# Loads, modulation and the first projections of a two-layer block as one program block on one Trainium2 core

## The chip, the core and the metric

The kernel runs on one core of one Trainium2 chip. The metric is the device time of one execution, in microseconds (us). The engines go by their names in the profile: PE (TensorE, matrix products; PEld is its weight load), DVE (VectorE), ACT (ScalarE), POOL (GpSimd) and SP (SyncE, which here issues all loads).

## The reference, cut to what matters

The program computes a whole model of two blocks (attention with a short convolution, a gated recurrence, then a second block of attention and feed-forward parts). The change is in its first 100 us: the modulation vectors of layer 0, the modulation of 512 tokens of x and of 256 context tokens, and the first projections.

```python
mod = silu(c) @ w_ada + b_ada          # per layer; the same for c_ctx
def modulate(h, shift, scale):
    return h * (1 + scale) + shift

def ab_layer(x, xc, mod, mod_c, w_in, w_out, sink, conv_w, ln_g, ln_b, row, col, ctx_out):
    shift, scale, gate = jnp.split(mod, 3, axis=-1)
    shift_c, scale_c, gate_c = jnp.split(mod_c, 3, axis=-1)
    q, k, v, g_a, xb, b_g, c_g, g_b = split_cols(modulate(x, shift, scale) @ w_in, widths)
    hc = modulate(xc, shift_c, scale_c)
    qc, kc, vc, g_ac, xbc, b_gc, c_gc, g_bc = split_cols(hc @ w_in, widths)
    ...
    x_new = layer_norm(DEEPNORM_ALPHA * x + gate * y, ln_g, ln_b)
```

(The line of `mod` is put in words of the same form; the rest is the reference's.) Shift and scale are needed before the first projection, `gate` only behind the output projection.

## The kernel before, in words

**Layout.** Activations lie with the 1024 model columns on partitions: 8 tiles (k = 0 to 7) of 128 partitions, each with 768 tokens (512 of x, 256 of context). A weight unit is 128x2048 f32 (1 MB); of `w_in` it holds two output tiles of 128 columns.

**Products in three parts.** Each f32 operand is split in a high part, rounded by ACT (`split_high`), and a low part, the difference, by DVE (`split_low`). `product3` (L276 to L280) issues three matmuls: high by high, low by high, high by low. In a weight unit's split (`SplitStream`, L262 and L268) the operands are 128x2048, in an x tile's (`SplitTiles`, L288 and L291) 128x768. PE waits for the low part of a unit before its first tile.

**Stage 1, `stage_start` (L366).** SP issues v, cf, eight units of the ada weights (u = 0 to 7, into a ring of five places), the first unit of `w_in`, x and context in four chunks of two tiles each, four more ada units (u = 8 to 11) and the second unit of `w_in`. PE multiplies the twelve ada units (L423, 8 products of 32 weight columns by 256 each) and after every second unit turns a row of 512 results to partitions (`flip`, L412, four small products), from rows that ACT copied out of PSUM (`turn`, L441). Units 0 to 7 are shift and scale, 8 to 11 are `gate`. When the fourth flip is there, DVE adds the bias (L475), adds 1 to the scale (L487), splits the low part of the first `w_in` unit (L270), and then modulates: for each of 8 tiles one instruction of 128x512 for x and one of 128x256 for context (L494), with the low split of the tile before (L293) between. ACT makes the high parts (L289), and then multiplies X by ALPHA (L456, eight of 128x768). The last DVE instruction is the bias of `gate`.

**Stage 2, `stage_ab_in` (L503).** A list `tiles` sets PE's order: q 0 to 3, k, v, then ga, rotations "r", xb, cg, gb, bg. Tile i uses PSUM banks 2(i mod 4) and the next, and waits until tile i-4 has been taken out. A tile other than v runs all eight k of x (24 matmuls of 128x512), then all eight of the context (24 of 128x256). ACT takes q, k, v, ga, xb and gb out (L581), and one iteration ahead splits the next unit; DVE does rotations, cg and bg, and casts a constant block (L632). SP loads further units when a raw place is free.

**Between them** stands the end of one `nc.Block()` and the start of the next: every engine jumps to the next block when all have ended theirs. The rows of the trace call what ends that wait "PEq L383".

Of the kernel before, what the change touches and what calls it, by code (L numbers as in the profile page):

```python
# [90 lines left out]
class Sems:  # L91

    def __init__(self, nc, es, tag):
# [67 lines left out]
        assert len(self.range) == 62  # L161


def program(nc, d):
# [5 lines left out]
    with es:  # L170
# [181 lines left out]
        raw_cb = arena1[:, ab_mark:ab_mark + NCB]  # L352
# [13 lines left out]
        def stage_start():  # L366
# [3 lines left out]
            S, N = stage_sems()  # L370
            c = Carve(0, arena1)
# [4 lines left out]
            padded_, picks_ = c(KT * 32), c(2)  # L376
            cond_ = padded_.rearrange("p (k x) -> p k x", k=KT)
            rows = [ca[:, 0:512], ca[:, 512:1024]]
            arrived = w_arrived[7:12]
            chunks = [slice(2 * i, 2 * i + 2) for i in range(4)]  # L380
            tiles_in = SplitTiles(S, [yin[:, k, :] for k in range(KT)], xh, xl)

            with nc.Block() as block:  # L383
                @block.sync
                def _(sp):
                    def unit(u):
                        if u >= 5:
                            sp.wait_ge(S.used, u - 4)
                        sp.dma_start(ring[u % 5], d["w1"][U0["ada0"] + u]).then_inc(arrived[u % 5], 16)

                    sp.sem_clear(N.range)
                    sp.sem_clear(w_range)
                    sp.dma_start(v1[:, :], d["v1"]).then_inc(S.load, 16)
                    sp.dma_start(cf[:, :], d["cf"]).then_inc(S.load2, 16)
                    for u in range(8):
                        unit(u)
                    ab_stream.fetch(sp, src_ab, 0)
                    for i, ks in enumerate(chunks):
                        sp.dma_start(X[:, ks, 0:L], d["xT"][:, ks, :]).then_inc(x_arrived[i], 16)
                        sp.dma_start(X[:, ks, L:T], d["ctxT"][:, ks, :]).then_inc(x_arrived[i], 16)  # L400
                    for u in range(8, 12):
                        unit(u)
                    ab_stream.fetch(sp, src_ab, 1)
                    sp.wait_ge(S.load, 16)
                    sp.wait_ge(S.load2, 16)

                @block.tensor
                def _(pe):
                    def flip(b):
                        pe.wait_ge(S.act_out, b + 1)  # L410
                        for j in range(4):
                            last = nc.tensor.matmul(PS[:, 6 + b // 4, 8 * b + 2 * j:8 * b + 2 * j + 2],  # L412
                                                    rows[b % 2][:, j * P:(j + 1) * P], picks_, start=True, stop=True)
                        last.then_inc(S.flipped, 1)

                    for u in range(12):
                        pe.wait_ge(arrived[u % 5], 16 * (u // 5 + 1))
                        if u == 0:
                            pe.wait_ge(S.act_step, 1)
                        w = ring[u % 5].rearrange("p (k n) -> p k n", k=KT)  # L420
                        for k in range(KT):
                            g = slice(32 * (k % 4), 32 * (k % 4) + 32)
                            last = nc.tensor.matmul(PS[g, u // 2, (u % 2) * 256:(u % 2 + 1) * 256],  # L423
                                                    cond_[:, k, :], w[:, k, :], start=(k < 4), stop=(k >= 4))
# [5 lines left out]
                        if u == 7:  # L430
                            flip(3)
# [3245 lines left out]
```

## Time and profile before

| what | value |
|---|---|
| median of 3 runs | 2468.87 us (2467.23 to 2468.99) |
| the profiled execution's own time | 2468.88 us |
| its span | 2467.1 us |
| PE busy | 2275.9 us, 92% of the span |
| DVE, ACT, POOL busy | 60%, 44%, 11% |
| mean granted clock of TensorE | 0.971 of full speed |
| first of 40 slices (61.7 us each) | PE 5 tenths, clock 7 tenths, DMA 8 tenths, 344 GB/s |

The profiled execution stands at the median of the runs, and its own time is 1.8 us above its span. Share of busy time says where an engine is used; what sets the length of a stretch is read from its waits and its order.

### The profile page before, as it was taken

How to read it: one execution, taken by the hardware profiler on the slowest of the kernel's cores; microseconds unless marked ns; L12 is line 12 of the kernel's file. 1: busy time of each engine (PE TensorE's matmuls, PEld its weight loads, DVE VectorE, ACT ScalarE, POOL GpSimd, SP SyncE). 2: the span in 40 equal slices, each digit the busy share in tenths (PEclk: the TensorE clock that was granted, in tenths of full speed). 3: DMA queues.
4: the chain of work that ended last, by engine and by line, in shares of the span. 5: the costliest groups of instructions: out<-in, count | busy, mean ns of one | idle time of the engine just before them, and what ended most of it. 6: DMA issues, size and time to landing. Idle time of an engine off the chain costs nothing. (4 is left out here: it accounts for less than half of the span.)

```text
span 2467.1 us, 36146 instructions
## 1 busy us (share of the span) xinstructions
PE 2275.9 (92%) x15278; PEld 1875.4 (76%) x15278; DVE 1470.0 (60%) x2225; ACT 1085.9 (44%) x1728; POOL 275.1 (11%) x147
## 2 busy tenths in 40 slices
PE   5999889789999978798899999999998899999997
PEld 3988767578888867677588888886786588888876
DVE  3133484748797795547667666347457667666255
ACT  3111373547667673435634334244336634334253
POOL 0000101513223150101001000001101010000011
PEclk7999999889999998899999999999999999999999
DMA  8112105311111112231022222331230012222321
GB/s 344 73 52 69 35 2 196 112 58 48 60 52 52 52 61 91 87 120 35 5 94 86 103 103 86 111 114 57 91 132 18 18 69 86 103 102 86 111 103 52
DMA packets 35201, 205.19 MB, mean 83 GB/s; under 512 B 3936, under 2 KB 5472, under 8 KB 14816
## 3 DMA queue, kind: packets, MB, share of 16 engines
q1 hardware_dynamic: 35040, 202.88, 23.2%
q8 instruction: 121, 1.98, 0.3%
q14 instruction: 40, 0.33, 0.0%
HBM read 200.77 MB, written 2.10 MB: 82 GB/s over the span
## 5 line engine op out<-in xcount | busy, mean ns | idle before, releaser
L278 PE MATMUL ps<-a_high,w_high 128*128 128x512 f32 (+1 forms) x1680 | 627.5, 373 | 38.5 <-DVE a_low L2550 18.6
L279 PE MATMUL ps<-a_low,w_high 128*128 128x512 f32 (+1 forms) x1680 | 619.1, 369 | 0.0
L280 PE MATMUL ps<-a_high,w_low 128*128 128x512 f32 (+1 forms) x1680 | 618.6, 368 | 0.0
L278 PEld LDWEIGHTS ps<-a_high,w_high 128*128 128x128 f32 x1680 | 318.2, 189 | 102.1 <-issue 18.4
L2168 DVE TENSOR_TENSOR w_low<-raw_ring,w_high 128x2048 fp32r<-128x2048 f32 x102 | 234.9, 2303 | 262.6 <-ACT w_high L2162 257.9
L279 PEld LDWEIGHTS ps<-a_low,w_high 128*128 128x128 f32 x1680 | 318.4, 190 | 53.6 <-issue 1.4
L280 PEld LDWEIGHTS ps<-a_high,w_low 128*128 128x128 f32 x1680 | 318.3, 189 | 52.7
L2162 ACT ACTIVATE w_high<-raw_ring 128x2048 fp32r<-128x2048 f32 x102 | 195.3, 1915 | 369.2 <-PE ps L280 282.0
L278 PE MATMUL ps<-x_high,place_high 128*128 128x512 f32 (+1 forms) x704 | 251.6, 357 | 9.9 <-POOL place_low L270 7.9
L279 PE MATMUL ps<-x_low,place_high 128*128 128x512 f32 (+1 forms) x704 | 246.0, 349 | 0.0
L280 PE MATMUL ps<-x_high,place_low 128*128 128x512 f32 (+1 forms) x704 | 245.4, 349 | 0.0
L278 PEld LDWEIGHTS ps<-x_high,place_high 128*128 128x128 f32 x704 | 135.4, 192 | 30.1 <-POOL place_low L270 8.8
L2964 POOL TENSOR_TENSOR arena<-arena 128x512 f32<-128x512 f32 (+1 forms) x36 | 56.3, 1563 | 865.4 <-ACT arena L3169 788.4
L279 PEld LDWEIGHTS ps<-x_low,place_high 128*128 128x128 f32 x704 | 135.5, 192 | 17.0 <-issue 0.7
L280 PEld LDWEIGHTS ps<-x_high,place_low 128*128 128x128 f32 x704 | 135.1, 192 | 17.4
L270 POOL TENSOR_TENSOR place_low<-place_raw,place_high 128x1024 fp32r<-128x1024 f32 x40 | 111.7, 2798 | 287.7 <-ACT place_high L266 287.7
L3421 DVE TENSOR_TENSOR arena<-ps,arena 128x1024 f32<-128x1024 f32 x44 | 53.9, 1224 | 133.3 <-PE ps L280 133.2
L3256 ACT ACTIVATE arena<-arena 128x512 f32<-128x512 f32 x44 | 27.9, 634 | 157.9 <-DVE arena L3443 157.9
L278 PE MATMUL ps<-x_high,ab_high 128*128 128x256 f32 (+1 forms) x256 | 87.9, 343 | 0.7 <-PEq L698 0.7
L279 PE MATMUL ps<-x_low,ab_high 128*128 128x256 f32 (+1 forms) x256 | 86.2, 337 | 0.0
L280 PE MATMUL ps<-x_high,ab_low 128*128 128x256 f32 (+1 forms) x256 | 86.1, 336 | 0.0
L2775 ACT ACTIVATE arena<-ps,arena 128x128 f32<-128x128 f32 (+3 forms) x128 | 66.0, 534 | 43.4 <-DVE arena L2828 43.1
(393 smaller groups left out, 4043.8 us busy)
## 6 DMA issues: line engine op xcount, KB each, us to landing
raw_ring<-w_dram SPq DMA_DIRECT2D x110, 1024.0 KB, 4.9
arena<-w_dram SPq DMA_DIRECT2D x26, 1024.0 KB, 8.1
place_raw<-wc_dram SPq DMA_DIRECT2D x48, 512.0 KB, 3.6
place_raw<-w_dram SPq DMA_DIRECT2D x11, 1024.0 KB, 5.0
ab_raw<-w_dram SPq DMA_DIRECT2D x10, 1024.0 KB, 4.9
x<-xT_dram SPq DMA_DIRECT2D x4, 512.0 KB, 13.9
out_dram<-x SPq DMA_DIRECT2D x1, 2048.0 KB, 7.2
arena<-r_dram SPq DMA_DIRECT2D x2, 992.0 KB, 6.0
```

The costliest lines, as they stand in the source:

```text
L270: (nc.gpsimd if by_pool else nc.vector).tensor_tensor(self.low(n), self.raw(n), self.high(n).bitcast(f32), O.subtract)\
L278: nc.tensor.matmul(out, wh, xh, start=start, stop=False)
L279: nc.tensor.matmul(out, wh, xl, start=False, stop=False)
L280: return nc.tensor.matmul(out, wl, xh, start=False, stop=stop)
L2162: nc.scalar.activation(self.high(n), self.raw(n), A.Copy).then_inc(w_hi, 1)
L2168: nc.vector.tensor_tensor(self.low(n), self.raw(n), self.high(n).bitcast(f32), O.subtract)\
L2775: last = nc.scalar.activation(pr[:, u % 3, g, c_ * w:(c_ + 1) * w], region(u)[:, g, c_ * w:(c_ + 1) * w], A.Exp, bias=st_bias[:, u, i:i + ...
L2964: nc.gpsimd.tensor_tensor(sq[:, 0:2, ts], sq[:, 0:2, ts], sq[:, k:k + 2, ts], O.add)\
L3256: nc.scalar.activation(hc[:, j % 2, 0, :], hc[:, j % 2, 0, :], A.Silu)\
L3421: nc.vector.tensor_tensor(hs[:, j % 2, :, :], tile2(PAIR[j % 4]), rstd[:, 1, :].unsqueeze(1).to_broadcast([P, 2, L]), O.mult)\
```

## The change

The two stages become one block, `stage_ab_in`. In it:

- The list of tiles is now q0, q1, q2, "m", q3, "f", k, v, and the rest as before. "m" is the products of ada units 8 to 11 (`gate`), into the two PSUM banks of its place in the list, from which ACT copies 128x1024 into `mod_rows`; "f" is their two flips, and DVE adds the bias.
- q0 and q1 are computed together, k outermost: when the low part of x tile k is there, PE does for both tiles the three 512-token and the three 256-token products of that k.
- DVE modulates x only. It does tiles 0 and 1, then the low split of the first `w_in` unit, then the low split of tile 0, and goes on with tile 2. ACT modulates the context (`context`, an Identity with scale and bias, 128x256), one tile ahead of its high split.
- The eight multiplications by ALPHA go among the evictions of the first projections, two for each of tile places 1 to 4.
- SP issues the second `w_in` unit ahead of ada units 8 to 10; unit 11 has a place inside the modulated tiles 4 to 6 and waits until all eight tiles are split; the third unit of `w_in`, and the constants `ca` and `sink`, come before it, the constant `cb` behind it. `cb` lies where the modulated tiles 0 to 3 were, so ACT waits for its cast before it writes ga 0.
- A set of twelve semaphores (`FirstSems`, `F`) serves what was stage 1.

```diff
-        def stage_start():
+        def stage_ab_in():
             S, N = stage_sems()
+            F = FirstSems(nc, es)
...
+            gate_place = arena1[:, yin_at + 4 * T:yin_at + 4 * T + UNIT]
+            places = [(ring[u % 5], u % 5, u // 5 + 1) for u in range(8)]
+            places += [(ring[3], 3, 2), (ring[4], 4, 2), (ring[2], 2, 3), (gate_place, 0, 3)]
...
+            tiles = ([("q", j) for j in range(3)] + [("m", 0), ("q", 3), ("f", 0), ("k", 0), ("v", 0), ("ga", 0), ("r", 0), ("ga", 1), ("r", 1),
...
                     ab_stream.fetch(sp, src_ab, 0)
                     for i, ks in enumerate(chunks):
                         sp.dma_start(X[:, ks, 0:L], d["xT"][:, ks, :]).then_inc(x_arrived[i], 16)
                         sp.dma_start(X[:, ks, L:T], d["ctxT"][:, ks, :]).then_inc(x_arrived[i], 16)
-                    for u in range(8, 12):
-                        unit(u)
                     ab_stream.fetch(sp, src_ab, 1)
...
+                    for u in (8, 9, 10):
+                        unit(u, (4, 5, 8)[u - 8])
                     ab_stream.load(sp, src_ab, RAW, RAW + 1)
                     sp.dma_start(ca, d["ca"]).then_inc(S.load, 16)
                     sp.dma_start(nsink, d["sink"]).then_inc(S.load, 16)
+                    sp.wait_ge(F.operand, KT)
+                    unit(11, 6)
                     sp.dma_start(raw_cb, d["cb"]).then_inc(S.load2, 16)
                     ab_stream.load(sp, src_ab, RAW + 1, 13 + RAW + 1)
...
+                    for k in range(KT):
+                        tiles_in.tile(pe, k)
+                        for i in range(2):
+                            ns = slice(i * P, (i + 1) * P)
+                            for a, b in ((0, L), (L, T)):
+                                last = product3(wide(i)[:, a:b], wh[:, k, ns], wl[:, k, ns], xh[k][:, a:b], xl[k][:, a:b],
+                                                k == 0, k == KT - 1)
...
+                        if t[0] == "m":
+                            for u in range(8, 12):
+                                last = mod_unit(u, 2 * (i % 4) + (u - 8) // 2)
+                            last.then_inc(S.pe_tile, 1)
+                            continue
+                        if t[0] == "f":
+                            pe.wait_ge(S.act_out, count(("m", 0)))
+                            flip(4, 2 * (i % 4))
+                            flip(5, 2 * (i % 4)).then_inc(S.pe_tile, 1)
+                            continue
...
+                    def context(k):
+                        if k % 2 == 0:
+                            act.wait_ge(x_arrived[k // 2], 32)
+                        nc.scalar.activation(yin[:, k, L:T], X[:, k, L:T], A.Identity, bias=modv(0, 0, 1, k),
+                                             scale=modv(0, 1, 1, k)).then_inc(F.kept, 1)
...
+                    ab_stream.split_high(act, u0)
+                    act.wait_ge(F.mixed, 1)
+                    context(0)
+                    for k in range(KT):
+                        if k < KT - 1:
+                            context(k + 1)
+                        act.wait_ge(F.kept, k + 1)
+                        act.wait_ge(F.dve_out, k + 1)
+                        tiles_in.split_high(act, k)
...
+                        if 1 <= i < 5:
+                            for k in range(2 * i - 2, 2 * i):
+                                nc.scalar.mul(X[:, k, :], X[:, k, :], ALPHA)
...
-                    ab_stream.split_low(dve, 0)
-                    for k in range(KT + 1):
-                        if k < KT:
-                            if k % 2 == 0:
-                                dve.wait_ge(x_arrived[k // 2], 32)
-                            for who, (a, b) in enumerate(((0, L), (L, T))):
-                                nc.vector.tensor_scalar(yin[:, k, a:b], X[:, k, a:b], modv(0, 1, who, k),
-                                                        modv(0, 0, who, k), O.mult, O.add).then_inc(S.dve_out, 1)
-                        if k:
-                            tiles_in.split_low(dve, k - 1)
+                    for k in range(KT + 1):
+                        if k < KT:
+                            if k % 2 == 0:
+                                dve.wait_ge(x_arrived[k // 2], 32)
+                            nc.vector.tensor_scalar(yin[:, k, 0:L], X[:, k, 0:L], modv(0, 1, 0, k), modv(0, 0, 0, k),
+                                                    O.mult, O.add).then_inc(F.dve_out, 1)
+                        if k == 1:
+                            ab_stream.split_low(dve, u0)
+                        if k:
+                            tiles_in.split_low(dve, k - 1)
```

**Place 1: DVE, from the scale's added 1 to the second x tile's low part.** `place_low` is the low part of the first `w_in` unit, `arena<-x,mod` a modulation. Before, and then in the changed kernel:

```order
L487 TENSOR_SCALAR mod<-mod 128x16
L270 TENSOR_TENSOR place_low<-place_raw,place_high 128x2048
L494 TENSOR_SCALAR arena<-x,mod 128x512
L494 TENSOR_SCALAR arena<-x,mod 128x256
L494 TENSOR_SCALAR arena<-x,mod 128x512
L494 TENSOR_SCALAR arena<-x,mod 128x256
L293 TENSOR_TENSOR x_low<-arena,x_high 128x768
```

```order
L632 TENSOR_SCALAR mod<-mod 128x16
L638 TENSOR_SCALAR arena<-x,mod 128x512 x2
L292 TENSOR_TENSOR place_low<-place_raw,place_high 128x2048
L315 TENSOR_TENSOR x_low<-arena,x_high 128x768
L638 TENSOR_SCALAR arena<-x,mod 128x512
L315 TENSOR_TENSOR x_low<-arena,x_high 128x768
```

The weight unit's low split moved behind two modulations, and those of the context left DVE.

**Place 2: PE, at the start of the projections and around "m".** Before, the last flips, the jump to the next block and the first products:

```order
L423 MATMUL ps<-arena 32x256 x32
L412 MATMUL ps<-arena 128x2 x8
L383 UNCONDITIONAL_BRANCH
L539 UNCONDITIONAL_BRANCH
L278 MATMUL ps<-x_high,place_high 128x512
L279 MATMUL ps<-x_low,place_high 128x512
L280 MATMUL ps<-x_high,place_low 128x512
```

In the changed kernel the start, and then the place of "m" between q2 and q3:

```order
L476 MATMUL ps<-arena,padded 32x256 x8
L482 MATMUL ps<-picks,arena 128x2 x4
L300 MATMUL ps<-x_high,place_high 128x512
L301 MATMUL ps<-x_low,place_high 128x512
L302 MATMUL ps<-x_high,place_low 128x512
L300 MATMUL ps<-x_high,place_high 128x256
```

```order
L302 MATMUL ps<-x_high,ab_low 128x256
L476 MATMUL ps<-arena,padded 32x256 x32
L300 MATMUL ps<-x_high,ab_high 128x512
L301 MATMUL ps<-x_low,ab_high 128x512
L302 MATMUL ps<-x_high,ab_low 128x512
```

The four `gate` units and both jumps left the front of the projections; the units stand behind the third projection tile.

**Place 3: SP, from the last chunk of context on.** Before, and then in the changed kernel:

```order
L400 DMA x<-ctxT_dram 128x2x256
L389 DMA arena<-w_dram 128x2048 x4
L251 DMA ab_raw<-w_dram 128x2048
L383 UNCONDITIONAL_BRANCH
L529 UNCONDITIONAL_BRANCH
L531 ISA
L251 DMA place_raw<-w_dram 128x2048
L533 DMA arena<-ca_dram 128x1024
L534 DMA arena<-sink_dram 128x8
L535 DMA arena<-cb_dram 128x2560
```

```order
L453 DMA x<-ctxT_dram 128x2x256
L273 DMA ab_raw<-w_dram 128x2048
L442 DMA arena<-w_dram 128x2048 x3
L273 DMA place_raw<-w_dram 128x2048
L458 DMA arena<-ca_dram 128x1024
L459 DMA arena<-sink_dram 128x8
L442 DMA arena<-w_dram 128x2048
L462 DMA arena<-cb_dram 128x2560
```

The second `w_in` unit moved ahead of the `gate` units, and the last of these behind the third `w_in` unit and two constants.

## Rows read from the trace of the kernel before

**Rows 1.** PE's waits from 53 to 262 us: engine, line, waited for, total, times, longest.
```profile
PE ps L278 <- PEq L383: 1.3, 1, 1.3
```

**Rows 2.** Busy time by stretch: length, PE, PEld, DVE, ACT, POOL, clock, DMA share, GB/s.
```profile
53.60:72.10 18.50, 18.45 (x96) 16.07 (x97) 2.29 (x1) 2.72 (x2) 0.00 (x0) 0.90 0.55 215
72.10:262.00 189.90, 189.90 (x1128) 167.74 (x1127) 55.89 (x51) 33.89 (x28) 0.00 (x0) 1.00 0.18 62
```

**Rows 3.** Timeline of PE, 20 to 73 us: start, length, work, idle before.
```profile
20.13 1.05 PE L412 MATMUL ps<-arena 128*128 128x2 f32 x8
...
24.22 1.07 PE L423 MATMUL ps<-arena 128*32 128x256 f32 x16 [2.04 <-DMA arena<-w_dram]
25.22 1.05 PE L412 MATMUL ps<-arena 128*128 128x2 f32 x8
...
29.21 1.87 PE L412 MATMUL ps<-arena 128*128 128x2 f32 x8 [0.72 <-ACT arena L441]
40.47 1.93 PE L423 MATMUL ps<-arena 128*32 128x256 f32 x16 [9.39 <-DMA arena<-w_dram]
...
50.48 1.87 PE L412 MATMUL ps<-arena 128*128 128x2 f32 x8 [0.52 <-ACT arena L441]
53.65 0.76 PE L278 MATMUL ps<-x_high,place_high 128*128 128x512 f32 x1 [1.30 <-PEq L383]
...
63.77 0.40 PE L278 MATMUL ps<-x_high,place_high 128*128 128x512 f32 x1
...
72.11 0.40 PE L278 MATMUL ps<-x_high,ab_high 128*128 128x512 f32 x1
```

**Rows 4.** Timeline of DVE, 31 to 38 us.
```profile
31.19 0.19 DVE L475 TENSOR_TENSOR mod<-ps,v 128x32 f32<-128x32 f32 x1 [25.18 <-PE ps L412]
...
31.62 2.29 DVE L270 TENSOR_TENSOR place_low<-place_raw,place_high 128x2048 fp32r<-128x2048 f32 x1
33.83 1.64 DVE L494 TENSOR_SCALAR arena<-x,mod 128x512 f32<-128x512 f32 x4
35.60 0.96 DVE L293 TENSOR_TENSOR x_low<-arena,x_high 128x768 fp32r<-128x768 f32 x1
36.48 0.87 DVE L494 TENSOR_SCALAR arena<-x,mod 128x512 f32<-128x512 f32 x2
37.26 0.95 DVE L293 TENSOR_TENSOR x_low<-arena,x_high 128x768 fp32r<-128x768 f32 x1
```

**Rows 5.** DMA queue of SP, 16 to 33 us: start and length of issues.
```profile
16.63 0.47 SPq L400 DMA_DIRECT2D x<-ctxT_dram  x1
...
27.98 1.09 SPq L400 DMA_DIRECT2D x<-ctxT_dram  x1
...
32.35 0.43 SPq L251 DMA_DIRECT2D ab_raw<-w_dram  x1
```

**Rows 6.** DMA issues at 16.6 us: count, KB each, us to landing.
```profile
x<-ctxT_dram SPq DMA_DIRECT2D x1, 256.0 KB, 15.0
```

**Rows 7.** DMA issues at 28.0 us, the same columns.
```profile
x<-ctxT_dram SPq DMA_DIRECT2D x1, 256.0 KB, 10.0
```

**Rows 8.** DMA issues at 32.4 us, the same columns.
```profile
ab_raw<-w_dram SPq DMA_DIRECT2D x1, 1024.0 KB, 18.0
```

**Rows 9.** Timeline of ACT, 28 to 50 us.
```profile
29.05 1.91 ACT L266 ACTIVATE place_high<-place_raw 128x2048 fp32r<-128x2048 f32 x1
34.73 1.62 ACT L289 ACTIVATE x_high<-arena 128x768 fp32r<-128x768 f32 x2 [3.77 <-DVE arena L494]
...
46.91 3.03 ACT L456 ACTIVATE x<-x 128x768 f32<-128x768 f32 x4
```

**Rows 10.** ACT groups by shape over the span: an activation with a scale operand.
```profile
L1785 ACT ACTIVATE x<-x,v 128x256 f32<-128x256 f32 x16 | 8.1, 587 | 3.5 <-DVE x L1623 3.5
```

**Rows 11.** Busy time by stretch, as in the second group, where the clock rises.
```profile
56.00:57.00 1.00, 1.00 (x4) 0.81 (x3) 1.00 (x1) 0.00 (x0) 0.00 (x0) 0.50 0.99 401
57.00:58.00 1.00, 1.00 (x5) 0.77 (x5) 0.86 (x1) 0.00 (x0) 0.00 (x0) 0.90 0.98 410
```

More of the change, by code:

```diff
@@ L161, in __init__, with sem @@
         assert len(self.range) == 62
+class FirstSems:
+    def __init__(self, nc, es):
+        def sem(name):
+            return es.enter_context(nc.semaphore(f"{name}_first"))
+        self.load = sem("load")
+        self.load2 = sem("load2")
+        self.ready = sem("ready")
+        self.used = sem("used")
+        self.act_step = sem("act_step")
+        self.act_out = sem("act_out")
+        self.flipped = sem("flipped")
+        self.mixed = sem("mixed")
+        self.dve_out = sem("dve_out")
+        self.kept = sem("kept")
+        self.rms_high = sem("rms_high")
+        self.operand = sem("operand")
 def program(nc, d):
@@ new lines, in flip, with first_flip @@
+                    def flip(b, bank):
+                        for j in range(4):
+                            last = nc.tensor.matmul(PS[:, bank, 8 * b + 2 * j:8 * b + 2 * j + 2],
+                                                    rows[b % 2][:, j * P:(j + 1) * P], picks_[:, :], start=True, stop=True)
+                        return last
+                    def first_flip(b):
+                        pe.wait_ge(F.act_out, b + 1)
+                        flip(b, 6).then_inc(F.flipped, 1)
+                    for u in range(8):
+                        if u == 0:
+                            pe.wait_ge(F.act_step, 1)
+                        mod_unit(u, u // 2).then_inc(F.used, 1)
+                        if u == 2:
+                            pe.wait_ge(F.ready, 2)
+                        if u % 2 == 0 and u >= 2:
+                            first_flip(u // 2 - 1)
@@ new lines, in _ @@
+                    first_flip(3)
+                    ab_stream.ready(pe, u0)
+                    wh, wl = [w.rearrange("p (k n) -> p k n", k=KT) for w in (ab_stream.high(u0), ab_stream.low(u0))]
+                    for k in range(KT):
[5 more added lines that the diff above has]
+                                                k == 0, k == KT - 1)
+                            if k == KT - 1:
+                                last.then_inc(S.pe_tile, 1)
@@ L541, in _ @@
                     for i, t in enumerate(tiles):
+                        if i < 2:
+                            continue
                         if i >= 4:
```

181 lines of the change are left out of this document (75 added, 106 removed).

## The prediction

> **What bounds the kernel now.** I read the waits of PE first, over the stage of the projections. From 53 to 262 us PE waits once, 1.3 us, and that is the jump into the block [rows 1]; from 72.1 us to 262 us it is busy 189.90 of 189.90 us at full clock [rows 2]. So this stage is a solid block of PE work: it ends earlier by what it starts earlier, and later by each microsecond of work put into it. Nothing else there has a say, since ACT is busy for 33.89 us and DVE for 55.89 us of the 189.90.
>
> Then the timeline of PE ahead of it. The last flip that shift and scale need starts at 29.21 us and takes 1.87 us, so DVE has them at 31.19 us; after it PE waits 9.39 us for an ada unit, works through the four `gate` units at their pace of arrival, and begins the first projection at 53.65 us [rows 3]. Between 31.1 and 53.65 us PE does only work that nothing in the projections needs. What the projections need comes from DVE and ACT. On DVE the reader is to see that the low part of x tile 0, the last thing that a first product needs, would be there at 35.60 + 0.96 = 36.56 us [rows 4], 17 us before PE looks at it.
>
> **The change, part by part.**
>
> *Start of the projections.* In the new order of DVE the shift and scale are ready at 31.62 us, as before. x tile 0 has landed at 16.63 + 15.0 = 31.63 us [rows 5, 6], so it isn't late by more than a hair. Two modulations of 128x512: four instructions, two of 512 and two of 256, took 1.64 us [rows 4]; with the two short ones gone I take 0.95 us (bounds 0.82, half of it, and 1.64). Then the weight unit's low part, 31.62 to 33.83 = 2.21 us from start to start, then the low part of tile 0, 0.96 us [rows 4]. 31.62 + 0.95 + 2.21 + 0.96 = 35.74 us, and with 0.1 us for the signal to PE **35.85 us** (35.7 to 36.6). ACT isn't the last here: its high part of the weight unit ends at 30.96 us [rows 9]; then come two contexts, each 0.59 us at most [rows 10], and one high part, 0.81 us (two took 1.62) [rows 9]: 31.6 + 1.18 + 0.81 = 33.6 us, hidden by DVE's 2.21 us. The start moves from 53.65 to 35.85: **-17.8 us**. The 1.30 us of the jump [rows 3] are in this term.
>
> *q0 and q1 by tiles of x.* The same 96 matmuls in another order, so their price is that of the two tiles before, 72.11 - 53.65 = 18.46 us; the second alone took 72.11 - 63.77 = 8.34 us [rows 3]. The difference is the low clock at the start: 0.50 in the stretch from 56 to 57, 0.90 in the next [rows 11]. It stays as it is if PE is again fed without a gap. PE wants at full clock 2 x 8.34 / 8 = 2.09 us for each x tile. DVE now gives one per modulation plus low part, at most 0.55 + 0.96 = 1.5 us (with the context in it, it was 37.26 - 35.60 = 1.66 us [rows 4]); ACT one per 0.59 + 0.81 = 1.4 us [rows 9, 10]. Both are shorter than 2.09. The last chunk of x lands at 27.98 + 10.0 = 38.0 us [rows 5, 7], and tile 6 is not modulated before 35.74 + 4 x 1.4 = 41.3 us. So **0**; bounds: 1.8 us less where the clock were full at once (18.46 - 16.68), 1.8 us more where the low stretch were twice as long. q2 would begin at 35.85 + 18.46 = 54.3 us.
>
> *The gate's work amid the projections.* It used to stand in a gap and now stands in solid PE work, so all of it counts. Four units: at full clock one started at 24.22 and the flips behind it at 25.22, so 1.00 us each [rows 3]. Two flips of four products, 1.05 us each [rows 3]. 4.0 + 2.1 = **+6.1 us**. At the low clock the rows say 1.93 us and 1.87 us [rows 3]: 11.5 us, the upper bound. I take the low price, as the engine comes out of 27 us of unbroken matmuls. Does PE wait there? "m" begins at 54.3 + 8.34 = 62.6 us. Unit 11 is the late one: behind x at 38.0 us there are ahead of it five units and `ca`, 5.8 MB, at 401 to 410 GB/s [rows 11] 14.2 us: 52.2 us, and 2.6 us for itself, 54.8 us. Its own wait, for all tiles split, ends at 35.74 + 7 x 1.4 = 45.5 us. So 7.8 us are to spare. "f" waits for ACT's copy of 1024 columns, with the whole of q3 (8.34 us) to hide in.
>
> *Second and third `w_in` unit.* The second landed at 32.35 + 18.0 = 50.4 us behind four `gate` units [rows 5, 8]. Even so late, 1.91 us of ACT [rows 9] and 2.29 us of DVE [rows 4] make 54.6 us against 54.3 us wanted; moved ahead of three of those units it lands some 8 us earlier. 0. The third is wanted at "k", 54.3 + 8.34 + 4.0 + 8.34 + 2.1 = 77.1 us, and ACT may split it from the end of q1 on. 0. Queued behind SP's new wait (until 45.5 us) are unit 11, `cb` and the fourth `w_in` unit, which is not read before ga 0, some 30 us later. 0.
>
> *ACT's multiplications by ALPHA.* Eight of 0.8 us (3.03 for four [rows 9]) move from beside the gate units to beside q1 to q3, where ACT has 0.8 us of eviction and 1.9 us of splitting per 8.34 us tile: 1.6 + 0.8 + 1.9 = 4.3. Tile i waits only for tile i-4. 0. The context halves on ACT are hidden as shown, and the cast of `cb` and its wait before ga 0 have DVE's idle time. 0.
>
> **Sum:** -17.8 + 6.1 = -11.7 us. Span 2467.1 - 11.7 = 2455.4, and 1.8 us around it, **2457.2 us**. The profiled execution (2468.88) stands at the median of the runs (2468.87), so no correction. Behind the stage all waits are on other engines, not on a time of day; the shift goes through whole.
>
> **The rivals.**
>
> *Gate's group dear.* The small products are at the low clock's price, or PE stops at the seams: -17.8 + 11.5 = -6.3, so 2462.6 us. For it: such units ran at either price in this trace. Against: each at the high price in the rows shown came after idle time of 0.52 to 9.39 us, and here none is due. 8%.
>
> *PE starved tile by tile, with the clock low (slower).* Place: q0 and q1, where PE now waits eight times for DVE. If modulation, context, high and low part run one behind another, 0.55 + 0.59 + 0.81 + 0.96 = 2.9 us a tile, PE at full clock (2.09 us) would wait 0.8 us each time, and the granted clock may stay at 0.50, as it does at 56 us [rows 11]. The point from which it decides is a supply above 2.09 us. At half clock the two tiles cost up to 33.4 us instead of 18.46 (+14.9), and "m" and "f" still low 5.4 more: -11.7 + 14.9 = +3.2 to +8.6, thus 2472.1 to 2477.5 us. For it: products that came in bursts, at 40.47 and 50.48 us, were at the low price [rows 3]. Against: the contexts run a tile ahead on another engine, and DVE did its longer list in 1.66 us a tile with ACT's high part beside it. At the low clock PE wants up to twice 2.09 us a tile, so it isn't starved there, and it is then fed as it was at 53.65 us. 4%. The Trainium skill, TensorE: Matmul & The Clock Gate, section on HAM oscillation, describes this pattern: an engine that waits for the next operand in each step along the contraction falls back to the slow clock and starts every step cold. By that rule the change would land in this rival; the trace has no such step-by-step feed with full-size products, so no row shows it.
>
> *Code and operands arrive late under a full DMA queue.* PE now starts while the queues move over 400 GB/s [rows 11], until about 57 us; before, the DMA share over q0 and q1 was 0.55 [rows 2]. Each such stop I price like the 1.30 us of the jump [rows 3]; two or three give 2460 to 2461 us. For it: instruction queues move in this program too, and share the DMA engines. Against: nothing of the kind stops PE in the stage before [rows 1]. 7%. The Trainium skill, Runtime: NRT & Kernel Launch, section Instruction fetch mechanics, says that an engine's code comes by its own DMA queue and is mostly hidden when sequential, while a taken jump out of the loaded pages stalls; by it this rival would cost nothing. No row here shows a fetch under load on PE while it is saturated.
>
> *The change gives nothing:* a later wait takes it all, 2468.9 us. PE's waits leave no room for it in this stage [rows 1, 2]. 2%.
>
> **How the numbers follow.** Forecast 79%, gate dear 8%, late code 7%, starved 4%, nothing 2%. The range reaches from the forecast less 1.8 us of clock and 0.9 us of run to run scatter, 2454.5, up to 2461.5, which takes in the clock's 1.8 us upward, 0.75 us of a later start and the third rival. A measurement of this kernel tells 0.2%, 4.9 us, from no change. Faster: 79 + 8 + 7 = 94, less 1 for mishaps added up: 93%. Same 3%, slower 4%.
>
> **What would show it.** First full-size product at 35.7 to 36.6 us; q2 at about 54.3; clock at full from about 40 us on; x tiles' low parts 1.3 to 1.5 us apart; 32 columns' products for `gate` in 4 us at about 62.6 us with no wait; no PE wait from 36 us to the stage's end, near 250 us. Wrong, if PE idles between x tiles, if the clock column reads 0.5 beyond 42 us, if "m" waits for unit 11, or if the stage ends at 262 us as before.

## The result and the profile after

| | before | changed |
|---|---|---|
| median | 2468.93 us (4 runs, 2467.23 to 2469.44) | 2455.86 us (4 runs, 2450.82 to 2456.95) |
| ratio | | 0.9943, 95% interval 0.9928 to 0.9958 |
| profiled execution | 2468.88 us, span 2467.1 | 2455.45 us, span 2453.6 |
| PE busy | 2275.9 us, 92% | 2270.5 us, 93% |

The changed kernel is 13 us faster, 0.57%. The forecast was 2457.2 us, in a range of 2454.5 to 2461.5. (In the three later sets of runs the kernel before had medians of 2467.1 to 2467.7 us, so 1 to 2 of the 13 us may be the scatter of these four runs.)

PE's waits from 30 to 252 us in the changed kernel (columns as in [rows 1]):

```profile
PE ps L300 <- DVE x_low L315: 4.8, 1, 4.8
PE ps L482 <- ACT arena L560: 0.7, 1, 0.7
```

Both lie ahead of the first projection. In the projections PE waits for nothing, as before [rows 1], and as the forecast needed: no wait between x tiles, none at "m" for unit 11, none at "f". The timeline of PE gives the places:

```profile
24.19 1.94 PE L476 MATMUL ps<-arena,padded 128*32 128x256 f32 x16 [1.89 <-DMA arena<-w_dram]
26.05 1.87 PE L482 MATMUL ps<-picks,arena 128*128 128x2 f32 x8
27.85 1.93 PE L476 MATMUL ps<-arena,padded 128*32 128x256 f32 x16
30.50 1.87 PE L482 MATMUL ps<-picks,arena 128*128 128x2 f32 x8 [0.72 <-ACT arena L560]
37.14 0.77 PE L300 MATMUL ps<-x_high,place_high 128*128 128x512 f32 x1 [4.77 <-DVE x_low L315]
...
55.48 0.40 PE L300 MATMUL ps<-x_high,ab_high 128*128 128x512 f32 x1
...
63.91 3.66 PE L476 MATMUL ps<-arena,padded 128*32 128x256 f32 x64
67.50 0.50 PE L300 MATMUL ps<-x_high,ab_high 128*128 128x512 f32 x1
...
75.99 1.84 PE L482 MATMUL ps<-picks,arena 128*128 128x2 f32 x16
77.69 0.49 PE L300 MATMUL ps<-x_high,place_high 128*128 128x512 f32 x1
```

The first full-size product starts at 37.14 us and not at 53.65 [rows 3]: 16.5 us earlier. q0 and q1 take 55.48 - 37.14 = 18.34 us, where they took 18.46. The gate's products take 67.50 - 63.91 = 3.59 us and its flips 77.69 - 75.99 = 1.70 us, 5.3 us together. 16.5 + 0.1 - 5.3 = 11.3 us.

The full price of the gate's work is a little higher. From the start of the third projection tile (55.48 us here, 72.11 before) to the first row of the attention stage (275.93 and 286.91 us, shown below) it is 220.45 us, against 214.80 before: 5.65 us. The part that the rows above don't show, 0.36 us, lies around them: the first product behind each group takes 0.50 and 0.49 us in place of 0.40. With it the sum closes: 16.51 + 0.12 - 5.65 = 10.98 us.

DVE shows how PE is fed:

```profile
32.48 0.19 DVE L619 TENSOR_TENSOR mod<-ps,v 128x32 f32<-128x32 f32 x1 [26.46 <-PE ps L482]
...
32.92 1.00 DVE L638 TENSOR_SCALAR arena<-x,mod 128x512 f32<-128x512 f32 x2
33.84 2.29 DVE L292 TENSOR_TENSOR place_low<-place_raw,place_high 128x2048 fp32r<-128x2048 f32 x1
36.04 0.95 DVE L315 TENSOR_TENSOR x_low<-arena,x_high 128x768 fp32r<-128x768 f32 x1
36.91 0.54 DVE L638 TENSOR_SCALAR arena<-x,mod 128x512 f32<-128x512 f32 x1
37.37 0.95 DVE L315 TENSOR_TENSOR x_low<-arena,x_high 128x768 fp32r<-128x768 f32 x1
```

Low parts come 37.37 - 36.04 = 1.33 us apart, against the 1.66 us of before [rows 4] and the 2.09 us that PE wants. ACT carries the context beside it (timeline of ACT):

```profile
38.30 0.59 ACT L565 ACTIVATE arena<-x,mod 128x256 f32<-128x256 f32 x1
38.87 0.84 ACT L311 ACTIVATE x_high<-arena 128x768 fp32r<-128x768 f32 x1
```

**Where the last 2 us came from.** The profiled spans differ by 13.5 us, not 11.3. The first row of PE in the later blocks tells where. Before:

```profile
286.91 2.00 PE L714 MATMUL ps<-arena 64*128 64x256 f32 x16 [2.36 <-PEq L528]
383.16 0.47 PE L278 MATMUL ps<-x_high,ab_high 128*128 128x512 f32 x1 [0.65 <-PEq L698]
...
1140.44 1.16 PE L2716 MATMUL ps<-arena 64*128 64x128 f32 x16 [1.96 <-PEq L2251]
```

Changed:

```profile
275.93 3.63 PE L769 MATMUL ps<-arena 64*128 64x256 f32 x16 [2.36 <-PEq L435]
369.81 0.47 PE L300 MATMUL ps<-x_high,ab_high 128*128 128x512 f32 x1 [0.65 <-PEq L753]
...
1126.78 1.16 PE L2770 MATMUL ps<-arena 64*128 64x128 f32 x16 [1.96 <-PEq L2305]
```

The attention stage starts 10.98 us earlier. It then took 96.25 us before and 93.88 us here, with the same instructions. The busy time by stretch shows the clock in it, before and then changed:

```profile
294.91:302.91 8.00, 6.87 (x30) 4.26 (x30) 6.62 (x20) 4.68 (x23) 0.01 (x1) 0.50 0.00 0
```

```profile
283.93:291.93 8.00, 6.18 (x36) 3.35 (x34) 6.96 (x22) 5.32 (x25) 0.00 (x0) 0.86 0.00 0
```

Before, 8 us of the stage's ragged start ran at 0.50; in the changed kernel the same place had 0.86. That difference belongs to the two executions and not to the change, as the experiments show: the same stretch, from the attention stage's start to the block that starts at 1140.44 us before, took 853.5 us before, 850.9 in the changed kernel, and between 847.3 and 854.6 us in the profiles of the twelve runs below, none of which touches it. What follows that stretch took 1326 to 1327 us each time. So about 11 us are the change's, and a single execution adds or takes some 3 us. (That the clock makes all of this variation isn't shown; the 8 us above are one place where it differs.)

### The profile page after: what moved, and what is told of

The parts are those of the page before. It is cut to its first block and busy times, and to the rows that moved or that the text cites. A ratio compares the mean times of both kernels' runs of the same rounds, so it can differ in the third digit from the quotient of the medians.

```text
span 2453.6 us, 36142 instructions
## 1 busy us (share of the span) xinstructions
PE 2270.5 (93%) x15278; PEld 1872.6 (76%) x15278; DVE 1468.0 (60%) x2217; ACT 1089.7 (44%) x1735; POOL 274.9 (11%) x147
## 5 line engine op out<-in xcount | busy, mean ns | idle before, releaser
L2829 ACT ACTIVATE arena<-ps,arena 128x128 f32<-128x128 f32 (+3 forms) x128 | 66.0, 534 | 43.5 <-DVE arena L2882 43.2
```

Of the source, the lines that this page charges most:

```text
L2829: last = nc.scalar.activation(pr[:, u % 3, g, c_ * w:(c_ + 1) * w], region(u)[:, g, c_ * w:(c_ + 1) * w], A.Exp, bias=st_bias[:, u, i:i + ...
```

## The experiments

Two theories at the start. **A:** the projections are one solid block of PE work, and the end moves with its start and with what is put into it. **B:** the gain is something else, the jump, or the going by x tiles alone, or the gate's move alone. "q2" is the start of the third projection tile, the attention stage's start is that of the rows above. "q0, q1 whole" takes back the going by x tiles and keeps the gate's move; "gate in front" takes back the gate's move and keeps the going by tiles. Ratios are to the kernel before on the same chip.

| run | median, us | ratio, 95% interval | first full-size product | q2 | attention stage |
|---|---|---|---|---|---|
| before | 2468.93 | | 53.65 | 72.11 | 286.91 |
| changed | 2455.86 | 0.9943 (0.9928 to 0.9958) | 37.14 | 55.48 | 275.93 |
| changed, again | 2455.05 | 0.9951 (0.9939 to 0.9963) | 37.18 | 56.82 | 277.27 |
| q0, q1 whole | 2466.12 | 0.9999 (0.9987 to 1.0010) | 46.16 | 65.36 | 285.81 |
| gate in front | 2467.91 | 0.9998 (0.9985 to 1.0010) | 53.69 | 72.13 | 286.93 |
| both undone | 2466.53 | 1.0000 (0.9991 to 1.0009) | 53.96 | 70.74 | 285.54 |
| context on DVE | 2456.92 | 0.9962 (0.9948 to 0.9977) | 36.79 | 56.40 | 276.84 |
| no gate products | 2452.27 | 0.9935 (0.9919 to 0.9952) | 37.08 | 55.38 | 271.99 |
| second unit late | 2455.29 | 0.9955 (0.9940 to 0.9970) | 37.11 | 55.29 | 275.73 |
| fill | 2454.76 | 0.9950 (0.9933 to 0.9967) | 35.82 | 52.83 | 273.27 |
| fill, again | 2454.46 | 0.9945 (0.9932 to 0.9957) | 35.68 | 54.18 | 274.62 |
| low part in pieces | 2454.34 | 0.9946 (0.9931 to 0.9961) | 35.76 | 55.05 | 275.50 |
| pieces and 3 fills | 2456.99 | 0.9955 (0.9940 to 0.9970) | 34.97 | 53.68 | 274.13 |
| pieces and 4 fills | 2453.93 | 0.9942 (0.9930 to 0.9954) | 35.78 | 53.54 | 274.00 |

The last two columns give a ruler that the clock doesn't blur: from q2 to the attention stage it is 214.80 us in the three kernels with the gate's work in front, 220.44 to 220.46 us in the ten that have it inside, and 216.61 us without its products. So the products cost 3.84 us there, the flips 1.81, and what else differs between executions lies ahead of q2 or behind the attention stage's start.

### q0 and q1 whole

```diff
-                    for k in range(KT):
-                        tiles_in.tile(pe, k)
-                        for i in range(2):
-                            ns = slice(i * P, (i + 1) * P)
-                            for a, b in ((0, L), (L, T)):
+                    tiles_in.tile(pe, KT - 1)
+                    for i in range(2):
+                        ns = slice(i * P, (i + 1) * P)
+                        for a, b in ((0, L), (L, T)):
+                            for k in range(KT):
...
```

> q0 and q1 are computed one after the other, once all eight tiles of x are split; everything else as changed. Theory (the start of PE's solid block sets the end): the low part of the last x tile ends at 46.0 us in the changed kernel, so the first full-size product moves from 37.1 to about 46.1 us, PE then has no wait, and the time is 9 us above the changed kernel's 2455.9, about 2464.8 us. Rival (the gain came from the gate's work and the jump, not from going by tiles): within 2 us of the changed kernel.

Measured 2466.12 us. Its timeline of PE:

```profile
46.16 0.76 PE L300 MATMUL ps<-x_high,place_high 128*128 128x512 f32 x1 [13.78 <-DVE x_low L315]
```

PE waits 13.78 us for the last x tile in place of 4.77 for the first: 9.0 us, as forecast, and the attention stage starts 9.9 us later (0.9 us of it is a longer stretch at the low clock: q0 and q1 took 65.36 - 46.16 = 19.20 us). The theory holds, and by its median the whole gain of the change is gone.

### The gate in front again

```diff
-            places += [(ring[3], 3, 2), (ring[4], 4, 2), (ring[2], 2, 3), (gate_place, 0, 3)]
+            places += [(ring[3], 3, 2), (ring[4], 4, 2), (ring[2], 2, 3), (ring[1], 1, 3)]
...
-            tiles = ([("q", j) for j in range(3)] + [("m", 0), ("q", 3), ("f", 0), ("k", 0),
+            tiles = ([("q", j) for j in range(3)] + [("q", 3), ("k", 0),
...
                     first_flip(3)
+                    for u in range(8, 12):
+                        mod_unit(u, 4 + (u - 8) // 2).then_inc(F.used, 1)
+                    for b in (4, 5):
+                        pe.wait_ge(F.act_out, b + 1)
+                        flip(b, 7).then_inc(F.flipped, 1)
```

Unit 11 is issued with units 8 to 10, and ACT takes the two rows out inside and behind its high parts, as before the change.

> The gate's four units and its flips go back in front of the first projection, inside the one block; x still goes by tiles. Theory: PE waits for the landing of unit 11 (about 48 us), flips by about 52 us, first full-size product near 52.5 us and not 37.1 us: 15.4 us later, and 5.3 us less inside the projections, so 10 us above the changed kernel, about 2466 us. The rest to the 2468.9 us of before, 1 to 3 us, is the jump. Rival (going by tiles is what gave the time): near 2456 to 2460 us.

Measured 2467.91 us. Its timeline of PE:

```profile
43.44 1.94 PE L475 MATMUL ps<-arena,padded 128*32 128x256 f32 x16 [10.28 <-DMA arena<-w_dram]
...
50.88 1.07 PE L475 MATMUL ps<-arena,padded 128*32 128x256 f32 x16 [1.42 <-DMA arena<-w_dram]
51.89 1.95 PE L481 MATMUL ps<-picks,arena 128*128 128x2 f32 x16
53.69 0.76 PE L300 MATMUL ps<-x_high,place_high 128*128 128x512 f32 x1
```

PE goes through the four units at their pace of arrival; the last comes at 50.88 us and not near 48, so the first product comes 1.2 us later than expected. It waits for loads that it doesn't need, and starts where it did before the change. Again the whole gain is gone. Nothing is left between this kernel and the one before (286.93 and 286.91 us at the attention stage), so the 1 to 3 us that the expectation put down to the jump aren't there.

### Both undone

Both edits together.

> Gate's work in front and q0 and q1 whole, in the one block. Theory (the projections start at the later of two things, the last x tile and the gate's flips, so each of the two edits alone gives next to nothing): the eighth low part is there before the gate's last flip, so going by tiles is worth nothing with gate in front, and the time is that of gate in front alone, 2466 to 2468 us, first full-size product near 53.7 us. Rival (each edit has a value of its own and they add): 8 to 10 us above gate in front alone, 2476 us.

Measured 2466.53 us, first full-size product at 53.96 us behind the flips:

```profile
50.60 1.62 PE L475 MATMUL ps<-arena,padded 128*32 128x256 f32 x16 [0.56 <-DMA arena<-w_dram]
52.15 1.95 PE L481 MATMUL ps<-picks,arena 128*128 128x2 f32 x16
53.96 0.47 PE L300 MATMUL ps<-x_high,place_high 128*128 128x512 f32 x1
```

Four kernels stand on two switches: neither edit 2466.5, going by tiles alone 2467.9, the gate's move alone 2466.1, both 2455.1 to 2455.9 us. Each alone gives nothing that can be measured, together 11 us. If the two edits had each a value of its own, undoing both would have cost more than undoing one; it doesn't. The start is the later of two things, the operands that PE asks for (one x tile or eight) and the gate's flips.

The clock has a part in these zeros:

| | start | q0 and q1 | gate's work behind q2 | attention stage |
|---|---|---|---|---|
| neither | 53.96 | 16.78 | | 285.54 |
| by tiles alone | 53.69 | 18.44 | | 286.93 |
| gate's move alone | 46.16 | 19.20 | 5.65 | 285.81 |
| both | 37.14 | 18.34 | 5.65 | 275.93 |

The gate's move alone does bring the start forward by 7.8 us, to the last x tile. It pays 5.65 us for its work inside, and q0 and q1 took 2.4 us more: they ran wholly at the full clock in the profile of "neither" and for 5.3 us at the low one here. With equal clocks this edit would be worth 7.8 - 5.65 = some 2 us (an estimate from these rows), and not nothing.

One block in place of two gives no difference here that can be measured (2466.5 beside 2467.1 us of the kernel before on the same chip, ratio 1.0000). The 1.30 us of the jump [rows 3] don't show, because the last unit's products start at 50.60 us where the last flips of before started at 50.48: these kernels keep the changed order of loads, in which the second `w_in` unit goes ahead of the gate's. What one block would be worth with the old order of loads was not tried.

### No gate products

```diff
-            tiles = ([("q", j) for j in range(3)] + [("m", 0), ("q", 3), ("f", 0), ("k", 0),
+            tiles = ([("q", j) for j in range(4)] + [("f", 0), ("k", 0),
...
                         if t[0] == "f":
-                            pe.wait_ge(S.act_out, count(("m", 0)))
+                            for u in range(8, 12):
+                                place, n, loads = places[u]
+                                pe.wait_ge(arrived[n], 16 * loads)
```

This kernel leaves out a part of the model (`gate`), so it can show only a price.

> The 64 matmul passes of the four gate units and ACT's copy behind them are left out, loads and flips stay (the flips turn older rows). Theory (every microsecond put into the solid block counts): the changed kernel's trace has 63.91 to 67.50 us for them, so 3.6 us under the changed kernel, about 2452.3 us. Rival (part of them lay in a gap or beside other work): less than 2 us.

The attention stage starts at 271.99 us, 3.94 us ahead of the changed kernel's, 3.84 of it behind q2, and the median is 2452.27, 2.8 to 3.6 us below its two medians (the intervals of the ratios overlap, so the landmark is what shows it). The profiled execution however has a span of 2453.3 us, only 0.3 us below: its stretch behind the attention stage's start took 854.6 us, the longest of all. The solid block counts each microsecond put in, and the rival's 2 us or less is out; one profile's span alone would have said the opposite.

### Context on DVE

```diff
-                    context(0)
                     for k in range(KT):
-                        if k < KT - 1:
-                            context(k + 1)
-                        act.wait_ge(F.kept, k + 1)
-                        act.wait_ge(F.dve_out, k + 1)
+                        act.wait_ge(F.dve_out, 2 * k + 2)
...
-                            nc.vector.tensor_scalar(yin[:, k, 0:L], X[:, k, 0:L], modv(0, 1, 0, k), modv(0, 0, 0, k),
-                                                    O.mult, O.add).then_inc(F.dve_out, 1)
+                            for who, (a, b) in enumerate(((0, L), (L, T))):
+                                nc.vector.tensor_scalar(yin[:, k, a:b], X[:, k, a:b], modv(0, 1, who, k), modv(0, 0, who, k),
+                                                        O.mult, O.add).then_inc(F.dve_out, 1)
```

> Context modulation back on DVE, everything else as changed. Theory: ahead of the first low part DVE has two instructions of 128x256 more, so the first full-size product comes 0.6 to 0.8 us later; then DVE gives a tile in 1.66 us, still under the 2.09 us that PE wants, so no wait behind it: 0.6 to 0.8 us above the changed kernel, about 2456.6 us. Rival (PE is starved tile by tile without ACT's help): PE waits between x tiles, 3 us or more.

Its timeline of DVE:

```profile
31.49 0.19 DVE L615 TENSOR_TENSOR mod<-ps,v 128x32 f32<-128x32 f32 x1 [26.02 <-PE ps L482]
...
35.69 0.95 DVE L315 TENSOR_TENSOR x_low<-arena,x_high 128x768 fp32r<-128x768 f32 x1
36.56 0.86 DVE L635 TENSOR_SCALAR arena<-x,mod 128x512 f32<-128x512 f32 x2
37.34 0.95 DVE L315 TENSOR_TENSOR x_low<-arena,x_high 128x768 fp32r<-128x768 f32 x1
```

From the bias to the start of the first low part it is 4.20 us against 3.56 with ACT's help, so 0.64 us; behind it 1.65 us a tile and no wait of PE. The bias itself came 1.0 us earlier in this execution, which hid it in the trace. The median is 1.1 us above the changed kernel's first. ACT's help is worth 0.6 us by the trace, and by time it can't be told.

### Second unit late

```diff
-                    ab_stream.fetch(sp, src_ab, 1)
                     for u in (8, 9, 10):
                         unit(u, (4, 5, 8)[u - 8])
+                    ab_stream.fetch(sp, src_ab, 1)
```

> The second unit of w_in is issued behind the gate's units 8 to 10, as before the change. Theory: it lands near 48 us and not 40.5 us, its two splits end near 52.5 us, and q2 wants it at 55.5 us, so no PE wait and the changed kernel's time, 2455.9 us within 1 us. Rival (the order of the loads matters): a wait at q2 of up to 2 us.

ACT waits for it until 47.47 us, DVE's low part runs from 49.42 to 51.71 us, and q2 starts at 55.29 us with no wait: no cost, as the forecast's zero for this edit says.

### Filling products

```diff
                     first_flip(3)
+                    for _ in range(5):
+                        nc.tensor.matmul(PS[:, 7, 0:256], ident, cf[:, 0:256], start=True, stop=True)
```

> Five products of 128x256 f32, whose result nobody reads, fill PE between the last flip and the first projection. Theory (the low clock at the start of the projections costs about 1.8 us, and comes from the idle time ahead of it): the granted clock is full at or soon after the first full-size product, q0 and q1 take about 16.8 us and not 18.3, 1.5 us under the changed kernel, about 2454.4 us. Rival (the filling delays the first product, or does not lift the clock): same or up to 1 us above.

Its timeline of PE:

```profile
30.92 4.61 PE L501 MATMUL ps<-cf 128*128 128x256 f32 x10
35.82 0.60 PE L300 MATMUL ps<-x_high,place_high 128*128 128x512 f32 x1 [0.29 <-DVE x_low L315]
36.26 0.40 PE L301 MATMUL ps<-x_low,place_high 128*128 128x512 f32 x1
```

From the second product on PE has its full clock, and q0 and q1 take 52.83 - 35.82 = 17.01 us in place of 18.34. The low clock hasn't gone: the ten passes of the fill ran at it (0.50 from 30 to 35.5 us), 4.61 us of work that nobody waits for. That the idle time ahead of the projections is its cause isn't shown by this. The median is 2454.76 us; with a ratio of 0.9950 against 0.9943 and 0.9951 of the changed kernel, time doesn't tell the two apart.

> The filling products once more, beside the changed kernel on this chip: 1.5 to 3 us under it, 2453 to 2454.5 us. If the variation of the clock in the later stages is larger than that, the two are not told apart by time, and only by the start of q2 (52.8 against 55.3 us).

The second time the last flip was so early (28.61 us) that the fill ended 1.07 us ahead of the operand, and the low clock lasted until about 39.1 us: q0 and q1 took 18.50 us. The operand didn't come as early as the bias (30.25 us), since DVE had to wait for the load of x tile 0:

```profile
31.46 1.00 DVE L640 TENSOR_SCALAR arena<-x,mod 128x512 f32<-128x512 f32 x2 [0.82 <-DMA x<-ctxT_dram]
```

So there is a floor under the start that no work on DVE or PE moves. Median 2454.46, 0.6 us under the changed kernel beside it and not the 1.5 to 3 expected:

> The changed kernel once more, for comparison on this chip: 2455.9 us within 1.5 us, first full-size product between 35.8 and 37.9 us, as the last ahead of it go at the high or the low clock.

2455.05 us. Its q0 and q1 took 19.64 us, since the low clock lasted from 37.18 to about 43.2 us (timeline of PE, then busy time by stretch as in [rows 2]):

```profile
37.18 0.77 PE L300 MATMUL ps<-x_high,place_high 128*128 128x512 f32 x1 [4.77 <-DVE x_low L315]
...
42.02 0.63 PE L302 MATMUL ps<-x_high,place_low 128*128 128x512 f32 x1
...
43.40 0.40 PE L301 MATMUL ps<-x_low,place_high 128*128 128x512 f32 x1
```

```profile
42.00:43.00 1.00, 1.00 (x5) 0.88 (x4) 1.00 (x3) 1.00 (x3) 0.00 (x0) 0.50 0.99 410
43.00:44.00 1.00, 1.00 (x7) 0.84 (x6) 1.00 (x2) 0.74 (x1) 0.00 (x0) 0.90 1.00 418
```

By the clock column the same program's first stretch of unbroken work was at the low clock for 3.2 us in one execution (until 40.3 us) and for 6.0 us in another.

### The low part in pieces

```diff
-                    ab_stream.ready(pe, u0)
...
                     for k in range(KT):
+                        if k in (0, 2):
+                            pe.wait_ge(F.ready, k // 2 + 3)
+                        if k == 4:
+                            ab_stream.ready(pe, u0)
                         tiles_in.tile(pe, k)
...
                         if k == 1:
-                            ab_stream.split_low(dve, u0)
+                            dve.wait_ge(w_hi, 1)
+                            low0(0, 512).then_inc(F.ready, 1)
                         if k:
                             tiles_in.split_low(dve, k - 1)
+                        if k == 1:
+                            low0(512, 1024).then_inc(F.ready, 1)
+                        if k == 2:
+                            low0(1024, 2048).then_inc(w_split, 1)
```

> The low part of the first w_in unit is made in three pieces, 512 columns ahead of the first x tile's low part, 512 and 1024 behind it. Theory (DVE's 2.29 us ahead of the first low part are on the path): the first full-size product comes 1.6 us earlier, at about 35.5 us, and PE has no wait behind it: 1.6 us under the changed kernel, about 2454.3 us. Rival: the pieces behind make a later x tile late, and PE waits 1 us or more there, so nothing is won.

Its timeline of DVE:

```profile
32.36 0.19 DVE L622 TENSOR_TENSOR mod<-ps,v 128x32 f32<-128x32 f32 x1 [26.81 <-PE ps L482]
...
33.72 0.68 DVE L627 TENSOR_TENSOR place_low<-place_raw,place_high 128x512 fp32r<-128x512 f32 x1
34.66 0.96 DVE L315 TENSOR_TENSOR x_low<-arena,x_high 128x768 fp32r<-128x768 f32 x1 [0.26 <-ACT x_high L311]
```

The first product starts at 35.76 us, 1.4 us earlier, with no wait behind it. (ACT's high part is now the last by 0.26 us.) But q2 starts only 0.4 us earlier, since the clock stayed low until about 41.1 us, 5.3 us of work in place of 3.2. In this execution what was won at the start was spent at the low clock; the changed kernel itself had 6.0 us of it in its second profile, so this isn't the pieces' doing. Median 2454.34 us, near the forecast's 2454.3 and, by the ratios, not apart from the changed kernel.

### Both, with three and with four filling products

> Both: three pieces, and three filling products. Theory: the two gains add, about 3 us under the changed kernel, 2452.8 us. Rival: PE at full clock from the start wants an x tile each 2.09 us, and with the pieces in between DVE comes late once or twice, which gives back up to 1 us.

With three, the bias came at 30.23 us, DVE waited 1.39 us for x tile 0, PE stood idle for 2.1 us behind the fill and was at the low clock until about 39.0 us; 2456.99 us, a miss, though the attention stage starts 1.8 us earlier than in the changed kernel.

> Three pieces of the low part and four filling products, one more than before, so that PE has no idle time ahead of the first product. Theory (the low clock follows the idle time, however short the fill before it; with three fills PE stood idle for 2.1 us and was slow until 38.95): first full-size product near 34.7 us and at full clock within 1 us, q2 near 52 us against 52.8 with the fill alone; 2453.5 us. Rival (DVE comes late with the pieces): PE waits of 0.3 to 1 us in the second and third tile, and q2 no earlier than 52.8 us.

The timeline of PE with four:

```profile
32.13 3.76 PE L501 MATMUL ps<-cf 128*128 128x256 f32 x8
35.78 0.77 PE L300 MATMUL ps<-x_high,place_high 128*128 128x512 f32 x1
...
37.63 0.33 PE L302 MATMUL ps<-x_high,place_low 128*128 128x256 f32 x1
37.80 0.39 PE L300 MATMUL ps<-x_high,place_high 128*128 128x512 f32 x1
```

Here PE had no idle time, and the clock still rose only at 37.7 us, 2 us into the projections and 5.6 us into the unbroken work that begins with the fill. So the theory that the low clock follows the idle time ahead doesn't hold. The bias came at 32.39 us this time, which puts the first product at 35.78 and not 34.7, and q2 at 53.54 and not 52. The rival's waits didn't come either. The median, 2453.93 us, is the lowest of the kernels that compute everything, 1.1 us under the changed kernel on the same chip, with intervals that overlap (0.9930 to 0.9954 and 0.9939 to 0.9963). The traces show 1.9 to 3.3 us at the attention stage's start, which takes in the scatter of the bias and of the clock; the time can't confirm it.

## Why the prediction was right

**The bound.** PE's block of projections as the only thing that counts: shown. Leaving out 3.6 us of it moved the attention stage by 3.9 us; starting it 9 us later moved that by 9.9. (The block doesn't end at 262 us, as the forecast's last signs have it: that was the edge of its rows. Its last product ended at 284.55 us before and at 273.57 in the changed kernel, 10.98 us earlier.)

**The start, forecast 35.85, measured 37.14 us.** The way from DVE's bias to the first product was forecast as 35.85 - 31.19 = 4.66 us and took 37.14 - 32.48 = 4.66 us. The 1.3 us lie ahead of it, in work that the change does not touch: the unit at 24.19 us and its flips went at the low clock (1.94 and 1.87 us) where those at 24.22 us had gone at the high one (1.07 and 1.05) [rows 3]. The forecast took the arrival of the bias from one execution as fixed; in the executions above it lies between 30.23 and 33.28 us. It also saw the second bound, x tile 0 landing at 31.63 us, and took it as late by a hair at most: where the bias was early, at 30.23 and 30.25 us, DVE waited 1.39 and 0.82 us for that tile. So a bias earlier than about 31 us wins nothing by itself.

**q0 and q1, forecast 0, measured -0.1 us**, and in the second execution +1.2 us, inside the 1.8 us allowed for the clock. That execution met one of the forecast's signs of being wrong, a clock column of 0.50 beyond 42 us, with PE busy all the time. The sign was a poor one: it tells how the clock fell, and not whether PE is starved.

**The gate's work, forecast +6.1, measured +5.65 us.** The four units ran in 3.59 us and not 4.0, the flips in 1.70 and not 2.1, and 0.36 us lie around them. The forecast's prices of one unit and one flip were read where each stood by itself; in a row each takes less.

**The loads.** No wait at q2, "m" or "k": shown by PE's waits. The placing of the second unit, costed at nothing, is worth nothing.

**The rivals.** The gate's group at the low clock's price: it ran at full clock. (The argument against it was thin: the forecast held that each group at the low clock's price came behind idle time, and the flips at 26.05 us in the changed kernel had none ahead of them.) PE starved tile by tile: supply 1.33 us against 2.09, no wait, and even with the context on DVE 1.65; in the first run with filling products PE was at full clock from its second product and didn't wait either. Code late under a full DMA queue: no stop of PE in the solid block, with DMA at its fullest until about 57 us. This rival was hardly put to the test, though: from 36 to 55 us the instruction queue moved one packet of 0.02 MB. The rule of the Trainium skill (TensorE: Matmul & The Clock Gate, HAM oscillation) found no hold, because its condition, a wait in each step, was absent; the page's own case also has waits several times as long as the 0.8 us priced for this rival.

**The sum.** -11.7 forecast for the block; -11.0 measured at the attention stage's start, -9.6 in the second profile. Two misses of opposite sign stand behind that nearness, the start 1.3 us too early and the gate's work 0.45 us too dear; the 1.3 us are the scatter of the bias, so how near the sum came is partly luck, and the mechanism is not. The median moved by 13.1 us, and by 12.1 in the second comparison. The forecast's sentence that the shift goes through whole is right as a mean and wrong for a single profile: the stretch behind it varies by 7 us from one execution to another.

## What to carry to other kernels

When a stage's start is the later of two things, cost an edit of one with the other in place: here each of the two edits alone gave nothing that could be measured and both together 11 us. Work moved out of a gap into a solid block is paid in full (5.65 us here), so it pays only if the gap closes by more. Read a gain of some microseconds off landmarks close to the change, ahead of it and behind it; the end of one span mixes in whatever varies in everything that follows.

## What the runs showed of the hardware

- How long PE stays at the low clock at the start of the projections isn't a property of the program: 3.2 and 6.0 us for the same kernel behind 4.77 us of idle time; 2 us with no idle time ahead of it; under 0.5 us with 0.29 us of idle time ahead; none in the profile of "both undone", which followed on its flips without idle time, and 3.4 us in that of "gate in front", which did the same.
- Filling products ran at the low clock themselves (0.50 over the 4.61 us of the first run's). Behind them it went on for under 0.5 us in one execution and for 1.9, 3.6 and 4.1 us in three others.
- The solid block repeats to 0.02 us: 220.44 to 220.46 us from q2 to the attention stage in ten profiles, at full clock and without a wait. The ragged stretch behind it, with the same instructions and PE busy for 89% of it, took 847.3 to 854.6 us, and the rest, with PE busy for 95%, 1326 to 1327 us.
- An ACT activation of 128x256 with scale and bias from memory took 0.59 us, as long as one with a scale had [rows 10], beside 0.84 us for a plain one of 128x768.
